# Down projection of the experts: two 256-column chunks in two ring slots multiplied as one 512-column moving operand

## What is computed

```python
def expert_choice_moe(h, w_router, w_gate, w_up, w_down):
    b, l, d = h.shape
    t = b * l
    xt = h.reshape(t, d)
    aff = jax.nn.softmax(jnp.matmul(xt, w_router, ...), axis=-1)
    cap = CAPACITY_FACTOR * t // N_EXPERTS      # 64 prompt tokens, 128 sample tokens an expert
    gates, idx = lax.top_k(aff.T, cap)
    xe = xt[idx]
    hid = jax.nn.silu(jnp.einsum('ecd,edf->ecf', xe, w_gate)) * jnp.einsum('ecd,edf->ecf', xe, w_up)
    ye = jnp.einsum('ecf,efd->ecd', hid, w_down)
    contrib = (gates[..., None] * ye.astype(jnp.float32)).astype(h.dtype).reshape(-1, d)
    y = jnp.zeros_like(xt).at[idx.reshape(-1)].add(contrib)
    return y.reshape(b, l, d)
```

## Time and profile before

| what | value |
|---|---|
| median of 3 runs | 3987.07 us (3985.03 to 3988.13) |
| profiled execution, span from first to last instruction | 3984.4 us |
| mean granted TensorE clock | 0.987 of full speed |
| TensorE busy | 3836.3 us |
| VectorE busy | 2677.0 us |
| ScalarE busy | 2108.6 us |
| memory traffic | 583.99 MB, 147 GB/s in the mean |

### The profile page before, as it was taken

The page is one execution under the profiler, slowest core; times in us unless marked ns, Lnnn a source line. Parts: engine busy times, 40 slices in busy tenths (PEclk is TensorE's granted clock), DMA queues, the critical chain, the costliest instruction groups (busy, mean ns, idle before and its releaser), DMA issues. The chain is left out here.

```text
span 3984.4 us, 75741 instructions
## 1 busy us (share of the span) xinstructions
PE 3836.3 (96%) x27408; PEld 3705.1 (93%) x27408; DVE 2677.0 (67%) x5533; ACT 2108.6 (53%) x3896; POOL 858.6 (22%) x1367
## 2 busy tenths in 40 slices
PE   8999999999989799999999999999997999999998
PEld 7989989999988699999999989999886999999998
DVE  6565664676665677777777757777536777777775
ACT  6544554555542255555555556555323556555654
POOL 5132230333330011111111133323000111211122
PEclk9999999999989899999999999999998999999999
DMA  3000001122124487887788731000436777877874
GB/s 109 10 21 7 25 16 36 49 66 69 52 97 153 141 252 235 254 249 245 241 251 253 240 86 51 31 24 16 149 130 206 237 248 247 256 240 247 253 244 130
DMA packets 492028, 583.99 MB, mean 147 GB/s; under 512 B 21537, under 2 KB 447521, under 8 KB 491809
## 3 DMA queue, kind: packets, MB, share of 16 engines
q1 hardware_dynamic: 473952, 522.44, 39.9%
q0 software_dynamic: 15680, 50.34, 6.0%
q10 hardware_dynamic: 2176, 8.39, 0.5%
HBM read 514.89 MB, written 66.22 MB: 146 GB/s over the span
## 5 line engine op out<-in xcount | busy, mean ns | idle before, releaser
L1687 DVE TENSOR_TENSOR wl<-raw,wh 128x2048 fp32r<-128x2048 f32 x384 | 879.1, 2290 | 283.0 <-ACT wh L1642 269.7
L1642 ACT CAST wh<-raw 128x2048 fp32r<-128x2048 f32 x384 | 732.8, 1908 | 24.3 <-DMA raw<-in_w_gate 22.1
L1786 PE MATMUL ps_g<-xT,wh 128*128 128x384 f32 x2048 | 595.0, 357 | 0.5 <-DVE xT L1693 0.5
L1786 PE MATMUL ps_u<-xT,wh 128*128 128x384 f32 x2048 | 594.8, 357 | 0.0
L1788 PE MATMUL ps_u<-xT,wl 128*128 128x192 f32 x2048 | 477.1, 253 | 0.0
L1788 PE MATMUL ps_g<-xT,wl 128*128 128x192 f32 x2048 | 477.1, 253 | 0.0
L151 PE MATMUL psP<-ring_high,hTh 128*128 128x384 f32 (+1 forms) x1344 | 460.2, 342 | 12.5 <-DVE ring_low L810 6.2
L153 PE MATMUL psP<-ring_high,hTl 128*128 128x384 f32 (+1 forms) x1344 | 441.6, 329 | 0.0
L152 PE MATMUL psP<-ring_low,hTh 128*128 128x384 f32 (+1 forms) x1344 | 441.2, 328 | 0.0
L1059 PEld LDWEIGHTS psO<-V,pT 128*128 128x128 f32 x3456 | 417.5, 192 | 20.4 <-issue 10.2
L1059 PE MATMUL psO<-V,pT 128*128 128x64 f32 x3456 | 415.6, 272 | 5.0 <-ACT pT L746 3.0
(11 more groups left out here) (212 smaller groups left out, 8725.5 us busy)
## 6 DMA issues: line engine op xcount, KB each, us to landing
raw<-in_w_gate SPq DMA_DIRECT2D x128, 1024.0 KB, 5.2
raw<-in_w_up SPq DMA_DIRECT2D x128, 1024.0 KB, 5.1
raw<-in_w_down SPq DMA_DIRECT2D x128, 1024.0 KB, 7.2
xb<-in_x SPq DMA_DIRECT2D x72, 256.0 KB, 2.8
out_y<-yb SPq DMA_DIRECT2D x24, 512.0 KB, 2.6
h_rows<-hb SPq DMA_DIRECT2D x24, 512.0 KB, 2.9
ring_raw<-in_w_a SPq DMA_DIRECT2D x24, 384.0 KB, 3.8
xb<-in_x SPq DMA_DIRECT2D x12, 512.0 KB, 4.7
```

The source lines that it names most:

```text
L1642: act.copy(wh[:, j % SPL], raw[:, j % RAW]).then_inc(w_high, 1)
L1687: dve.tensor_tensor(wl[:, j % SPL], raw[:, j % RAW], wh[:, j % SPL].bitcast(F32), ALU.subtract)\
L1786: both = lambda **fl: pe.matmul(ps[:, f, 0:2 * CAP], wh[:, j % SPL, k, fs], xT[:, k].rearrange("p h c -> p (h c)"), **fl)
```

## The change

For all experts but a layer's last, d0 and d1 are multiplied together, and so are d2 and d3. The moving operand is one access pattern over two neighbouring ring slots, `wh[:, slots, k]`: 2 runs of 256 columns, 2048 elements apart. The output is a whole bank of 512 columns. So a pair has 40 matmuls of 512 columns instead of 2 x 40 of 256, and the results are copied, added and scaled once a pair, 512 columns wide. Pairs use `ps_y` and `ps_u`. Both slots are released together at the pair's end (`used` + 2). ScalarE and VectorE split chunk d3 in step d0 as before; after the first pair's results they split the next expert's g0 and u0, after the second pair's results its g1. The third batch of transposes comes after the first pair. The counts that the semaphores are compared with are adapted. The last expert of a layer works as before.

```diff
+    PAIRS = NCH // 2
+    EV = 2 * NCH + PAIRS
...
-    yp = ph.sb("yp", [CAP_P, 2, 2, FC])
+    yp = ph.sb("yp", [CAP_P, 2, 2, 2 * FC])
...
-        return {"g": ps_g, "u": ps_u, "d": (ps_y, ps_g, ps_u)[c % 3]}[kind]
+        return {"g": ps_g, "u": ps_u, "d": (ps_y, ps_g, ps_u)[c % 3], "pair": (ps_y, ps_u)[c % 2]}[kind]
+
+    def step_of(j, last):
+
+        if j < 2 * NCH or last:
+            return j
+        return 2 * NCH + (j - 2 * NCH) // 2
+
+    def ends_step(j, last):
+
+        return j < 2 * NCH or last or (j - 2 * NCH) % 2 == 1
...
+            def pair_out(e, d):
+
+                act.wait_ge(used, e * N + 2 * NCH + 2 * d + 2 + SPL)
+                act.wait_ge(summed, e * EV + 2 * NCH + d + 1)
+                act.copy(yp[:, d, 0], banks("pair", d)[CAP_P:2 * CAP_P, 1, :]).then_inc(second_out, 1)
+
             def expert(e, last):
 
                 act.activation(dummy[:, :], ident[:, 0:1], ACT.Silu)
                 for j, (kind, c) in enumerate(chunks):
-                    nj, nxt = split_at(j)
-                    if not (nxt and last):
-                        high(e + nxt, nj)
+                    paired = kind == "d" and not last
+                    if paired and c % 2 == 1:
+                        pair_out(e, c // 2)
+                    if paired and c == 1:
+                        x_out(e + 1, [XB - 1])
+                    for ahead in ([j] if not paired or c == 0 else [j, j + 1] if c == 1 else [j] if c == 3 else []):
+                        nj, nxt = split_at(ahead)
+                        if not (nxt and last):
+                            high(e + nxt, nj)
+                    if paired:
+                        continue
...
+            def result(e, ps, step, n, b, cols):
+
+                if n == 0:
 
                     dve.wait_ge(added, e + 1)
-                ps, cols = banks("d", c), slice(c * FC, (c + 1) * FC)
...
+                w = cols.stop - cols.start
+                dve.wait_ge(second_out, e * EV + step + 1)
+                dve.tensor_tensor(yp[:, b, 1, 0:w], ps[0:CAP_P, 1, 0:w], yp[:, b, 0, 0:w], ALU.add).then_inc(joined, 1)
+                dve.tensor_scalar(cs[:, cols], ps[:, 0, 0:w], gate[:, bass.ds(e + 32, 1)], None, ALU.mult).then_inc(summed, 1)
+                dve.wait_ge(joined, e * PAIRS + n + 1)
+                dve.tensor_scalar(cp[:, cols], yp[:, b, 1, 0:w], gate[0:CAP_P, bass.ds(e, 1)], None, ALU.mult).then_inc(scaled, 1)
...
+            def down(e, ps, w, slots, first):
+                ways = slots.stop - slots.start
+                out = lambda h: ps[:, h, 0:w].rearrange("p (s f) -> p s f", s=ways)
+                for k in range(KD):
+                    if first and k in (0, KD - 2):
+
+                        pe.wait_ge(h_low, e * NCH + (NCH - 1 if k == 0 else NCH))
+                    fl = dict(start=(k == 0), stop=False)
+                    high, low, end = wh[:, slots, k], wl[:, slots, k], k == KD - 1
+                    pe.matmul(out(0), hT[:, k, S_HI], high, **fl)
+                    pe.matmul(out(0), hT[:, k, S_HI], low, start=False, stop=False)
+                    pe.matmul(out(1), hT[:, k, P_BOTH], high, **fl)
+                    pe.matmul(out(1), hT[:, k, P_BOTH], low, start=False, stop=end)
+                    ins = pe.matmul(out(0), hT[:, k, S_LO], high, start=False, stop=end)
+                return ins
...
                     pe.wait_ge(w_low, e * N + j + 1 + RAW)
...
+                    if not ends_step(j, last):
+                        continue
+
+                    pe.wait_ge(summed, e * EV + step_of(j, last) + (0 if kind == "d" and last else 1))
+                    if kind == "d" and last:
+                        ins = down(e, banks("d", c), FC, slice(j % SPL, j % SPL + 1), c == 0)
+                    elif kind == "d":
+                        ins = down(e, banks("pair", c // 2), 2 * FC, slice(j % SPL - 1, j % SPL + 1), c == 1)
...
-                    ins.then_inc(used, 1)
+                    ins.then_inc(used, 2 if kind == "d" and not last else 1)
                     if j == 2 * NCH - 1 and not last:
                         turn_x(e + 1, range(XB - 1))
-                    if j == 2 * NCH and not last:
+                    if j == 2 * NCH + 1 and not last:
                         turn_x(e + 1, [XB - 1])
```

More of the change, by code:

```diff
@@ L1652, in expert @@
                 for j, (kind, c) in enumerate(chunks):
-                    nj, nxt = split_at(j)
-                    if not (nxt and last):
-                        high(e + nxt, nj)
+                    paired = kind == "d" and not last
[9 more added lines that the diff above has]
+                        continue
                     if kind == "u":
-                        act.wait_ge(summed, e * N + j + 2)
+                        act.wait_ge(summed, e * EV + j + 2)
                         act.activation(sg[:, c % 2], gs[:, c % 2], ACT.Silu).then_inc(silu_done, 1)
                     act.wait_ge(used, e * N + j + 1 + SPL)
-                    act.wait_ge(summed, e * N + j + 1)
+                    act.wait_ge(summed, e * EV + j + 1)
                     ps = banks(kind, c)
                     if kind == "d":
-                        act.copy(yp[:, c % 2, 0], ps[CAP_P:2 * CAP_P, 1, 0:FC]).then_inc(second_out, 1)
+                        act.copy(yp[:, c % 2, 0, 0:FC], ps[CAP_P:2 * CAP_P, 1, 0:FC]).then_inc(second_out, 1)
                     else:
                         act.copy(second[:, j % 2], column_half(ps, 1)).then_inc(second_out, 1)
-                    if kind == "d" and c == 0 and not last:
-                        x_out(e + 1, [XB - 1])
                     if kind == "u":
@@ L1708, in expert @@
             def expert(e, last):
                 for j, (kind, c) in enumerate(chunks):
-                    nj, nxt = split_at(j)
-                    if not (nxt and last):
-                        low(e + nxt, nj)
+                    paired = kind == "d" and not last
+                    if paired and c % 2 == 1:
+                        d = c // 2
+                        result(e, banks("pair", d), 2 * NCH + d, d, d, slice(2 * d * FC, 2 * d * FC + 2 * FC))
+                    if paired and c == 1:
+                        x_out(e + 1, [XB - 1])
@@ L1713, in expert @@
+                    for ahead in ([j] if not paired or c == 0 else [j, j + 1] if c == 1 else [j] if c == 3 else []):
+                        nj, nxt = split_at(ahead)
+                        if not (nxt and last):
+                            low(e + nxt, nj)
+                    if paired:
+                        continue
                     if kind == "d":
-                        result(e, j, c)
+                        result(e, banks("d", c), j, c, c % 2, slice(c * FC, (c + 1) * FC))
                     else:
@@ L1766, in expert @@
                     pe.wait_ge(w_low, e * N + j + 1 + RAW)
[L1768 to L1777, removed]
-                            pe.matmul(ps[:, 0, 0:FC], hT[:, k, S_HI], low, start=False, stop=False)
-                            pe.matmul(ps[:, 1, 0:FC], hT[:, k, P_BOTH], high, **fl)
-                            pe.matmul(ps[:, 1, 0:FC], hT[:, k, P_BOTH], low, start=False, stop=end)
-                            ins = pe.matmul(ps[:, 0, 0:FC], hT[:, k, S_LO], high, start=False, stop=end)
+                    if not ends_step(j, last):
+                        continue
+                    pe.wait_ge(summed, e * EV + step_of(j, last) + (0 if kind == "d" and last else 1))
[3 more added lines that the diff above has]
+                        ins = down(e, banks("pair", c // 2), 2 * FC, slice(j % SPL - 1, j % SPL + 1), c == 1)
                     else:
+                        ps = banks(kind, c)
                         for f in range(FB):
```

17 lines of the change are left out of this document (4 added, 13 removed).

## The result

| | before | after |
|---|---|---|
| median | 3987.07 us (3984.97 to 3988.13, 5 runs) | 3954.68 us (3953.45 to 3957.86, 5 runs) |
| span of the profiled execution | 3984.4 us | 3952.9 us |

The ratio is 0.9922 with a 95% interval of 0.9912 to 0.9933: 32.4 us or 0.8% faster. The direction was right and the gain is twice the forecast 15.6 us.

The account below looks back on a forecast made before the run. TensorE's own time was taken to bound the expert stage. Wider matmuls were to save 15.6 us and every other term nothing: 3987.07 - 15.6 = 3971.5 us, range 3966 to 3984.

Parts of the forecast that it names:

- What bounds the kernel: Expert stage: only TensorE's own time counts, repeating every 57.37 us; other engines count only once they make it wait.
- The 512-column price: Pair matmuls: 233.5 ns each, taken from the output projection, against two of 120.0; 15.6 us less over 30 experts.
- The reading of the rows behind it: Matmul prices: 0.456 to 0.458 ns a column, so 256 columns pay only about 3 ns over the rate.
- The weight load: Down matmuls: the load is already hidden at 256 columns, so halving the number of loads brings little.
- The jump between runs: Moving operand in two runs, 2048 elements apart: taken as nothing, bounded above by 48 us of cost.
- Order, splits, ring, transposes and DMA: Expert stage: moved transposes, later splits, ring-slot releases and loads all stay hidden, costing nothing.
- g1: Second gate chunk on TensorE: its wait for the first chunk's sum hidden by 0.1 us; nothing, bound 6 us.
- Rival C: Inside each new matmul: 213 ns at the granted clock without excess, 64 us saved, 3923; chance 0.05.
- The range's lower end: Total of 3966 us, from a 512-column price a little under 232 ns (3987.1 - 20.4).

Follow-up runs that it names:

- r11_pad448: Changed kernel with 448 bytes of room ahead of the output projection's stationary operands, putting them a multiple of 512 bytes from the moving ones: 3948.62 us, ratio 0.9907.
- r9_bench: Changed kernel plus 13 blocks of 48 bare 512-column matmuls behind the last expert, with operands shifted 0 to 128 bytes: settled steps 226.7 to 234.3 ns.
- r12_shift: Changed kernel with 64 bytes of room ahead of the expert stage's stationary operand hT: 3970.99 us, ratio 0.9964.
- r1_bench: Changed kernel plus rows of 40 bare matmuls of each operand shape behind the last expert: 256 columns settled at 120.0 ns, 512 at 226.7 ns.
- r3_contiguous: Changed kernel with a pair's two ring slots interleaved, so the moving operand is one run of 512 contiguous columns: 3954.67 us, ratio 0.9919.
- r4_projection: Changed kernel with the output projection's 512-column moving operand as two runs of 256 columns, 512 elements apart: 3955.89 us, ratio 0.9921.
- r2_narrow: Changed kernel's pair schedule, but with the pair's matmuls as 80 of 256 columns again: 3985.48 us, ratio 0.9999.
- r6_late: Changed kernel with one more 512-column ScalarE copy (about 0.59 us) ahead of the split of the next expert's second gate chunk: 3967.97 us, ratio 0.9951.
- r5_bench: Changed kernel plus eight blocks of bare 512-column matmuls in different product orders, each behind eight transposes: all settled at 226.7 ns.

## Why the prediction was right or wrong

**What bounds the kernel: right.** The whole gain is in the expert periods, and outside them only the projection (r11_pad448, 4 to 6 us) answered to anything tried here.

**The 512-column price: wrong, the term that was mis-sized.** "Per pair step: 80 x 120.0 = 9.60 us before, 40 x 233.5 = 9.34 us after" used the projection's 233.5, with the smallest believed price at 232. It measured 226.7 in the pair. The 6.7 ns between are a property of where the projection's tensors lie to each other: r9_bench and r12_shift make them come, r11_pad448 makes them go. 2400 x 6.7 = 16 us, and the whole miss is 16.8.

**The reading of the rows behind it: wrong.** "At that rate 256 columns would be 117 ns: the narrow matmul pays only about 3 ns over the rate." The rate was made of two rows that each held something else: the 512 of the projection the 6.7 ns, and the 384 of the earlier trace rows the longer steps at a start: its stretch begins right behind transposes, the last four of its ten steps are 173 ns each, and r1_bench's block of 384 is 173.5. Both pushed the price per column up and left almost no fixed part. The prices are columns at 2.4 GHz plus 13.3 ns, so merging two saves 13.3.

**The weight load: the conclusion was wrong, the premise is not shown.** "At 256 columns the load is already hidden, so halving the number of loads brings little" missed that halving the number of matmuls, each with its load, saves 13.3 ns a time. Whether any of that is the load no run tells.

**The jump between runs at nothing: right** (r3_contiguous, r1_bench, r4_projection). **Order, splits, ring, transposes and DMA at nothing: right** (r2_narrow, and the times from the gate start above). **g1: right that it is hidden, by less than a quarter of a microsecond;** the slack is 0.22 us and not 0.1, since from the sum's end to TensorE it takes 0.05 us and not 0.22 (r6_late). The sum's end itself was right (+8.83, predicted +8.79).

**Rival C** was wrong about its 213 ns and right about its reason in part: of the 20 ns over the columns that it gave to the projection alone, 6.7 are the projection's and 13.3 everyone's. The range's lower end stood on 232 ns, a row of the same tensors as 233.5 and so no bound of its own; a bound by columns at 2.4 GHz plus what the 256-column rows pay (213.3 + 13.3) would have met the result: 2400 x 13.4 = 32 us.

Still open: what the 13.3 ns are; why the distance counts (32, 64, 96 and 128 bytes were tried, 256 not), and with its sign; why 448 and 480 columns cost more; and what sets the length of the unsettled start.

## What to carry to other kernels

Split the price of a matmul into slope and fixed part, from several widths on the same tensors and from settled steps, before valuing a merge; merging two saved the fixed part, 13.3 ns, once. A price from another stage carries that stage's places with it: here 6.7 ns, which a pad of 448 bytes took away. A slack that is worked out from measured durations is as good as its weakest term: here the handover between two engines, taken from another place, made 0.1 us of what was 0.22. Either is thin, and once it is gone, TensorE loses more than the time that it waits.

## What the runs showed of the hardware

- In these rows a float32r matmul with its own weight load, at the 2.4 GHz level, steps at 120.0, 146.7, 173.3 and 226.7 ns for 256, 320, 384 and 512 columns, but 206.5 and 216.8 for 448 and 480.
- A moving operand in two or four runs costs what one run does (226.7 or 226.5 ns).
- The distance between stationary and moving operand counts: a multiple of 512 bytes gave 226.7 ns, 32 to 128 bytes more or less gave 228.8 to 234.3 (r9_bench), and both operands shifted alike 226.7.
- Behind transposes the first step of a 512-column matmul is 312 to 324 ns and the next two to nine are 224 to 236 before they settle at 226.7 (r5_bench); behind 480-column matmuls nine steps are unsettled too (r1_bench).
- A stop of TensorE costs more than its idle time: g1 started 0.26 us later in r6_late, and a period was 0.44 us longer.
